# A router on un-normalised sums, ranks summed by TensorE, and weight loads begun ahead of the last norm

## The reference, cut to what matters

```python
h = layer_norm(ALPHA * h + m2 * (mixed @ w_out), ln_mix_g, ln_mix_b)   # post-norm
u = h * (1 + m4) + m3                                                  # modulation
logits = einsum('nd,de->en', u, w_router)       # 16 experts
aff = softmax(logits, axis=experts)
gate, idx = top_k(aff, 64)                      # each expert takes 64 tokens
xe = u[idx]
ye = (silu(xe @ w_g) * (xe @ w_u)) @ w_d * gate
h = layer_norm(ALPHA * h + m5 * scatter_add(idx, ye), ln_ffn_g, ln_ffn_b)
```

## Time and profile before

| | |
|---|---|
| median of 3 runs | 2962.73 us (2961.95 to 2963.7) |
| profiled execution, time | 2959.35 us |
| profiled execution, span | 2957.6 us |
| TensorE busy | 2730.9 us, 92% of the span |
| DVE busy | 1154.3 us, 39% |
| ACT busy | 823.6 us, 28% |
| POOL busy | 126.6 us, 4% |
| mean granted TensorE clock | 0.968 |
| read from memory | 596.90 MB, 203 GB/s over the span |
| chain that ended last | TensorE 75%, DMA 12%, DVE 8%, ACT 4% |

### The profile page before, as it was taken

How to read it: one execution, slowest core, us unless ns; L and a number is a source line. 1 busy time by engine, 2 the same in 40 slices (tenths; PEclk the granted TensorE clock), 3 DMA queues, 4 the chain that set the end, 5 groups by cost and what they waited for, 6 DMA issues and landing times.

```text
span 2957.6 us, 32708 instructions
## 1 busy us (share of the span) xinstructions
PE 2730.9 (92%) x13724; PEld 1797.5 (61%) x13724; DVE 1154.3 (39%) x1684; ACT 823.6 (28%) x1272; POOL 126.6 (4%) x124
## 2 busy tenths in 40 slices
PE   6998899998899979998988999999999999999998
PEld 4555444343368544433337777878778766787886
DVE  4464612111264351111226664323334577533333
ACT  2353311010032121110015424322232467532222
POOL 1210100000000110000001010000010000000000
PEclk8999899999999979999999999999999899999999
DMA  8870699999932079999992112232241300132220
GB/s 299 316 233 16 264 420 426 429 427 421 424 112 103 16 309 427 428 427 427 428 381 87 62 57 95 82 108 72 96 129 41 85 1 1 59 120 78 95 91 36
DMA packets 125651, 601.11 MB, mean 203 GB/s; under 512 B 7440, under 2 KB 12880, under 8 KB 100672
## 3 DMA queue, kind: packets, MB, share of 16 engines
q1 hardware_dynamic: 120128, 584.27, 50.0%
q0 software_dynamic: 5376, 14.75, 1.7%
HBM read 596.90 MB, written 2.10 MB: 203 GB/s over the span
## 4 chain that ended last, share of the span: by engine, by line
PE 75%; DMA 12%; DVE 8%; ACT 4%; issue 1%; POOL 0%; DVEq 0%; SPq 0%; ACTq 0%; POOLq 0%
PE psum L295 72%; DMA weight_ring<-in_w_exp_down 6%; PE psum L310 4%; ACT scratch L283 4%; DVE scratch L245 2%; DMA scratch<-in_w_exp_down 2%; DMA weight_ring<-in_w_exp_up 2%; DMA scratch<-in_w_exp_up 1%; DMA weight_ring<-in_w_mix_in 1%; DVE h L245 1%; DVE scratch L258 1%; DVE scratch L3650 0%; DVE scratch L1408 0%; DVE scratch L1826 0%; DVE scratch L278 0%
## 5 line engine op out<-in xcount | busy, mean ns | idle before, releaser
L295 PE MATMUL psum<-scratch,scratch 128*128 128x512 f32 (+12 forms) x9384 | 1882.0, 398 | 62.9 <-DVE scratch L245 21.8
L295 PEld LDWEIGHTS psum<-scratch,scratch 128*128 128x128 f32 (+3 forms) x9384 | 1380.0, 180 | 529.9 <-issue 207.2
L295 PE MATMUL psum<-weight_ring,scratch 128*64 128x512 f32 (+2 forms) x2752 | 647.5, 610 | 71.3 <-DMA weight_ring<-in_w_exp_down 27.6
L295 PEld LDWEIGHTS psum<-weight_ring,scratch 128*64 128x64 f32 (+2 forms) x2752 | 211.5, 141 | 462.7 <-issue 369.0
L283 ACT ACTIVATE scratch<-psum 128x512 f32<-128x512 f32 (+4 forms) x362 | 210.3, 581 | 999.7 <-PE psum L310 544.3
L245 DVE TENSOR_TENSOR scratch<-weight_ring,scratch 128x2048 fp32r<-128x2048 f32 (+2 forms) x110 | 241.9, 2199 | 485.3 <-ACT scratch L283 483.8
L283 ACT ACTIVATE scratch<-weight_ring 128x2048 fp32r<-128x2048 f32 (+2 forms) x122 | 218.8, 1793 | 571.8 <-PE psum L295 548.6
L245 DVE TENSOR_TENSOR scratch<-scratch,psum 128x512 f32<-128x512 f32 x92 | 63.3, 688 | 521.9 <-PE psum L295 520.4
L245 DVE TENSOR_TENSOR scratch<-scratch,scratch 128x512 fp32r<-128x512 f32 (+12 forms) x355 | 199.1, 561 | 61.5 <-ACT scratch L283 43.0
L310 PE MATMUL psum<-consts,scratch 128*128 128x128 f32 x1116 | 169.6, 294 | 55.5 <-DVE scratch L245 38.9
L310 PEld LDWEIGHTS psum<-consts,scratch 128*128 128x128 f32 x1116 | 135.0, 164 | 116.0 <-issue 48.1
(11 more groups left out here) (106 smaller groups left out, 728.1 us busy)
## 6 DMA issues: line engine op xcount, KB each, us to landing
weight_ring<-in_w_exp_gate SPq DMA_DIRECT2D x44, 2048.0 KB, 15.8
weight_ring<-in_w_exp_down SPq DMA_DIRECT2D x44, 2048.0 KB, 14.2
weight_ring<-in_w_exp_up SPq DMA_DIRECT2D x43, 2048.0 KB, 15.7
weight_ring<-in_ffn_w SPq DMA_DIRECT2D x28, 2048.0 KB, 7.8
weight_ring<-in_w_mod SPq DMA_DIRECT2D x24, 2048.0 KB, 9.5
scratch<-in_w_exp_up SPq DMA_DIRECT2D x21, 2048.0 KB, 16.1
scratch<-in_w_exp_gate SPq DMA_DIRECT2D x20, 2048.0 KB, 15.8
scratch<-in_w_exp_down SPq DMA_DIRECT2D x20, 2048.0 KB, 13.6
```

What stands on the lines that cost most here:

```text
L295: ins = T.eng.matmul(out, lhsT, rhs, start=start, stop=stop)
```

## The change

- **Router on sums.** TensorE turns the un-normalised sum `z` as soon as it stands, half by half, and ACT copies it out plainly (one operation for each half). The gains and the modulation are folded into the router once (`router_dve`), and mean and root are applied to the 16 logits of each token behind the product (`shift_dve`, `logits_dve`). The router is now the stationary operand, 32 columns wide and zero-padded, in four column groups of the array side by side (`logits_pe`); one more small product adds the four groups (`sum_pe`).
- **Order in the mixer.** TensorE turns the tile before between the two output products of a tile. Tile 3's root is taken first and its norm and split only behind the exponential, whose table ACT loads ahead by one small operation. The norm is written to `h`; the parts for the gather are made of the normed tile without gain and bias, and `xeT` is scaled by `turned_scale` and `turned_shift`. Gain and bias of tiles 2 and 3 are applied on DVE in the experts.
- **Ranks.** The marks themselves are transposed; the threshold is on 128x64; a triangle of ones and ones sum them in four products, and a multiplication masks them.
- **Loads.** In layer 0 the first gate pieces go to the two `more` slots at once, without waiting for the mixer's end; the lent slots follow with the first up pieces. In layer 1 the loads still wait for the mixer's end, which now stands ahead of the last norm on ACT and DVE and ahead of the last split on POOL.
- **Halves.** Turning the first gathered rows and the first expert product wait for one half each instead of both.

```diff
@@ MixerOut
     def pe(self, T):
         self.k.fence(T, self.before)
         spread_pe(self.k, T, self.key, self.norm.diag)
         for t in range(NT):
-            project_out_tile(self.k, T, self.key, self.xT, t)
+            project_out_tile(self.k, T, self.key, self.xT, t, halves=(0,))
+            if t == 0:
+                self.next.rows_w_pe(T)
             if t >= 2:
-                self.next.logits_pe(T, t - 2)
+                self.next.sum_pe(T, t - 2)
             if t:
-                self.next.turn_pe(T, t - 1)
+                for q in range(2):
+                    self.next.turn_pe(T, t - 1, q)
+            project_out_tile(self.k, T, self.key, self.xT, t, halves=(1,))
+            if t:
+                self.next.logits_pe(T, t - 1)
+        for q in range(2):
+            self.next.turn_pe(T, NT - 1, q)
+        T.end(self.key)
+        self.next.sum_pe(T, NT - 2)
+        self.next.logits_pe(T, NT - 1)
+        self.next.sum_pe(T, NT - 1)
         if self.rest:
             self.rest.first_pe(T)
-        self.next.turn_pe(T, NT - 1)
-        T.end(self.key)
-        self.next.logits_pe(T, NT - 2)
-        self.next.logits_pe(T, NT - 1)
     def act(self, A):
...
+        for t in range(NT - 1):
+            self.norm.norm_act(A, t)
+            self.next.split_act(A, t)
+            for q in range(2):
+                self.next.turned_out(A, t, q)
+            self.next.part_out(A, t)
+        for q in range(2):
+            self.next.turned_out(A, NT - 1, q)
+        self.norm.root_act(A, NT - 1)
         A.end(self.key)
+        self.next.exp_act(A)
+        self.norm.normal_act(A, NT - 1)
+        self.next.split_act(A, NT - 1)
     def dve(self, V):
...
+        for t in range(NT):
+            self.norm.stats(V, t)
+            if t >= 2:
+                self.next.logits_dve(V, t - 2)
+            if t == NT - 1:
+                V.end(self.key)
+            self.norm.finish(V, t)
+            if t == 0:
+                self.next.rows_w_dve(V)
+            self.next.shift_dve(V, t)
+            if 0 < t < NT - 1:
+                self.norm.gained(V, t - 1)
+        self.next.part_out(V, NT - 1)
+        self.next.logits_dve(V, NT - 2)
+        self.next.logits_dve(V, NT - 1)
     def pool(self, G):
...
         for t in range(NT):
-            self.norm.norm_pool(G, t)
-            if t:
-                self.next.pool_row(G, t - 1)
-        G.end(self.key)
-        self.next.pool_row(G, NT - 1)
+            if t == NT - 1:
+                G.end(self.key)
+            self.next.pool_row(G, t)
+            if t and t < NT - 1:
+                self.norm.norm_pool(G, t - 1)
@@ Experts
-    def turn_pe(self, T, t):
+    def turn_pe(self, T, t, q):
-        T.wait_ge(*k.at(self.before, "norm", t))
+        T.wait_ge(*k.at(self.before, "sum", t, q))
...
-    def fused_dve(self, V):
+    def router_dve(self, V):
...
         tt(V, self.turned_scale, gain, self.scale, ALU.mult)
         tt(V, self.turned_shift, bias, self.scale, ALU.mult)
-        tt(V, self.turned_shift, self.turned_shift, self.shift, ALU.add, (self.key, "fused"))
+        tt(V, self.turned_shift, self.turned_shift, self.shift, ALU.add)
+        fill(V, self.router_w, 0.0)
+        w = self.router_w[:, :, 0:E]
+        tt(V, w, self.router, self.turned_scale.unsqueeze(2).to_broadcast([P, NC, E]), ALU.mult, (self.key, "router"))
+        tt(V, self.router_b, self.router, self.turned_shift.unsqueeze(2).to_broadcast([P, NC, E]), ALU.mult)
+        reduce(V, self.w_sums[:, 0:E], w.rearrange("p c e -> p e c"), ALU.add)
+        reduce(V, self.w_sums[:, E:2 * E], self.router_b.rearrange("p c e -> p e c"), ALU.add, (self.key, "router sums"))
+        V.eng.tensor_tensor_scan(self.triangle, k.ones, k.ident, 0.0, ALU.mult, ALU.add).then_inc(*V.mark((self.key, "triangle")))
+        reduce(V, self.pick, k.ident.rearrange("p (g e) -> p e g", g=4)[:, 0:E, :], ALU.add, (self.key, "pick"))
+    def rows_w_pe(self, T):
...
+        mm(T, bank[:, 0:2 * E], k.ones, self.w_sums, True, True, ("full", key, "rows"))
+    def shift_dve(self, V, t):
+        stt(V, self.shifted[:, t, :], self.w_rows[:, 0:E], self.source.mv[:, t, 1:2], self.w_rows[:, E:2 * E], ALU.mult, ALU.add)
     def logits_pe(self, T, t):
...
+        bank = k.psum.take(T, (key, "part", t), (0, 7))
+        for r in range(2):
+            for g in range(4):
+                c = 4 * r + g
+                mm(T, bank[32 * g:32 * g + 32, 0:P], self.router_w[:, c, :], self.uT[:, t % 2, c, :], r == 0, r == 1,
+                   *([("full", key, "part", t)] if c == NC - 1 else []))
+    def part_out(self, lane, t):
...
+        evac(lane, self.part[:, t % 2, :], k.psum.of((key, "part", t))[:, 0:P], ("free", key, "part", t))
+    def sum_pe(self, T, t):
...
+        mm(T, bank[:, 0:E], self.part[:, t % 2, :], self.pick, True, True, ("full", key, "logits", t))
+    def logits_dve(self, V, t):
...
+        stt(V, self.logits[:, t, :], k.psum.of((key, "logits", t))[:, 0:E], self.source.r[:, t, :], self.shifted[:, t, :],
+            ALU.mult, ALU.add, ("free", key, "logits", t))
     def turned_out(self, lane, t, q):
...
+        evac(lane, self.uT[:, t % 2, 4 * q:4 * q + 4, :], k.psum.of(job).rearrange("p (c n) -> p c n", c=4), ("free", *job))
+    def exp_act(self, A):
+        act(A, self.warm, self.k.ones[:, 0:1], ACT.Exp)
+        A.wait_ge(*self.k.at(self.key, "logits less max"))
+        act(A, self.aff, self.aff, ACT.Exp, (self.key, "exp"))
     def sync(self, Y):
         k, d = self.k, self.k.dram
-        if not self.rest:
+        if self.rest:
+            k.ring.next_in(len(k.ring.base), MORE_SLOTS)
+        else:
             k.ring.widen(Y, self.before)
-        k.ring.lend(Y, self.before)
+            k.ring.lend(Y, self.before)
         for what, e in self.order():
...
+                if self.rest and (name, e) == ("w_exp_up", 0):
+                    k.ring.lend(Y, self.before)
+                    k.ring.next_in(len(k.ring.base) + MORE_SLOTS, LENT_SLOTS)
     def pe(self, T):
...
-        T.wait_ge(*k.at(key, "ranks"))
+        T.wait_ge(*k.at(key, "marked"))
+        bank = k.psum.take(T, (key, "marks"), self.ROUTING)
+        for t in range(NT):
+            tr(T, k, bank[:, t * E:(t + 1) * E], self.work[0:E, t * P:(t + 1) * P],
+               *([("full", key, "marks")] if t == NT - 1 else []))
+        T.wait_ge(*k.at("free", key, "marks"))
         bank = k.psum.take(T, (key, "rank"), self.ROUTING)
-        for t in range(NT):
-            tr(T, k, bank[:, t * E:(t + 1) * E], self.work[0:E, t * P:(t + 1) * P],
+        T.wait_ge(*k.at(key, "triangle"))
+        chosen = self.chosen.rearrange("p t e -> p (t e)")
+        mm(T, bank[:, 0:NT * E], self.triangle, chosen, True, False)
+        for t in range(1, NT):
+            mm(T, bank[:, t * E:NT * E], k.ones, chosen[:, 0:(NT - t) * E], False, t == NT - 1,
                *([("full", key, "rank")] if t == NT - 1 else []))
     def dve(self, V):
...
-        ts(V, work, work, 0.0, None, ALU.is_lt, None)
-        V.wait_ge(*k.at("loaded", f"ones{self.layer}"))
-        V.wait_ge(*V.last())
-        V.eng.tensor_tensor_scan(affT, self.ones[0:E, :], work, 0.0, ALU.mult, ALU.add).then_inc(*V.mark())
-        tt(V, work, work, affT, ALU.mult, (key, "ranks"))
+        V.wait_ge(*k.at("full", key, "marks"))
+        ts(V, self.chosen, k.psum.of((key, "marks"))[:, 0:NT * E].rearrange("p (t e) -> p t e", e=E), 0.0, None, ALU.is_lt, None,
+           ("free", key, "marks"))
         V.wait_ge(*k.at("full", key, "rank"))
-        copy(V, self.rank, k.psum.of((key, "rank"))[:, 0:NT * E].rearrange("p (t e) -> p t e", e=E), ("free", key, "rank"))
+        tt(V, self.rank, k.psum.of((key, "rank"))[:, 0:NT * E].rearrange("p (t e) -> p t e", e=E), self.chosen, ALU.mult,
+           ("free", key, "rank"))
...
         self.turned_dve(V, 0)
+        for t in (NT - 2, NT - 1):
+            self.source.gained(V, t)
...
     def turned_pe(self, T, p):
-        for half in range(2):
-            T.wait_ge(*k.at("free", key, "rows", p, half))
         for q in range(2):
+            T.wait_ge(*k.at("free", key, "rows", p, q))
...
     def up_pe(self, T, e):
-        for q in (range(2) if e in (0, 2, 4, 6) else ()):
-            T.wait_ge(*k.at("free", key, "pair", e // 2, q))
...
+                if w == "w_exp_gate" and c % 4 == 0 and e in (0, 2, 4, 6):
+                    T.wait_ge(*k.at("free", key, "pair", e // 2, c // 4))
```

167 lines of the change are left out of this document (84 added, 83 removed).

## The result

The changed kernel takes 2942.31 us (2940.75 to 2944.66, four runs) against 2962.34 for the kernel before in the same series: ratio on record 0.9942, interval 0.993 to 0.9954 (the quotient of the two medians is 0.9932, so the record's ratio gives the smaller gain). The forecast was 2950.7 and a range of 2944.5 to 2958.5. So the direction was right and the gain, 17 us by that ratio and 20 by the medians, was larger than the 12 forecast. The profiled execution went from a span of 2957.6 to one of 2938.7, 18.9 less.

A forecast was written before the change was run, and what follows sets the result against it. Each expert layer was taken to end when its unbroken train of weight loads ends. Gains of 7.4 us (layer 1) and 4.6 (layer 0) sum to -12.0, giving a median of 2950.7, range 2944.5 to 2958.5.

The forecast's parts named there:

- Ahead of E: Mixer work before E, the end of its last output product: E moves +2.0 us per layer (+1.0 to +3.8).
- E to the stage's end: From the last output product to ACT's root, which releases the loads: 3.05 us.
- E to MAX8: Routing from the last output product to the first MAX8: 8.3 us against 16.8 before.
- Marks to gather: Ranks, from the marks' transposes to the gather's issue: 2.6 us warm, 3.5 cold, 3.8 before; layer 0 loses 1 us waiting.
- Halves: Turning gathered rows by halves takes DVE's copy of half 1 and its latency off the path: -0.8 us.
- Warm gather: Layer 0's first gather product may stay at 2.4 GHz: 0 to -2.5 us.
- First expert product: Start of the experts in both layers: -6.5 - 0.3 - 0.8 = -7.6 us.
- Train of layer 0: Expert weight loads: start 5.2 us earlier, 2.8 dry, dips of 1.0 gone; 3.4 to 6.2, taken as -4.6.
- Train of layer 1: Expert weight loads start at 1046.5 against 1053.90: -7.4 us.
- more than forecast: Rival: router product near 0.5 us and the warm clock give 2946.9 or lower; chance 0.09.
- three signs of failure: E moving over 4 us, TensorE waiting at a turn or sum inside output products, trains running dry again behind 480.
- Only layer 1 gains: Rival: layer 0's dry spell is longer, as when piece 11 or 13 meets a late first expert; 2955.3, chance 0.12.

The follow-up runs named there:

- e1: Changed kernel with layer 0's loads as before: all behind the mixer's end, in the old order of slots; 2942.59 us, ratio 0.9942.
- e2: Changed kernel with layer 0's new order of slots but no loads issued ahead of the mixer's end; 2941.97 us, ratio 0.994.
- f1: Changed kernel with another order of slots in layer 0, so that piece 11 waits for piece 4, not 5; 2941.86 us, ratio 0.9947.
- f3: Changed kernel with extra products that nothing reads in TensorE's pauses of layer 1's routing; 2943.8 us, ratio 0.9957.
- f4: Changed kernel with f1's slots, layer 0's gates ahead of the last modulation pieces, unread products in both layers, layer 1's first three loads early; 2939.58 us, ratio 0.9942.
- e3: Changed kernel with the mixer's end mark back behind tile 3's norm and split; 2949.39 us, ratio 0.9962.
- e6: Changed kernel with both halves awaited before turning and before the first expert product, as before; 2945.6 us, ratio 0.9962.
- e7: Changed kernel with the router product the old way round, without the four column groups, their copy and sum; 2955.05 us, ratio 0.9988.
- e8: Changed kernel with layer 0's modulation product moved behind the four transposes of the affinities; 2942.58 us, ratio 0.9951.
- e5: Changed kernel with the ranks as before: threshold, scan and product on DVE, transposes of the ranks; 2942.52 us, ratio 0.995.
- e4: Kernel before with only layer 0's new order and early issue of loads, without the new mixer; 2960.88 us, ratio 1.0004.

## Why the forecast had the right mechanism and too small a gain

Step by step, with the forecast's terms:

- **Ahead of E, +2.0 us.** Measured +0.3 and +2.6 in the profiled pair, +0.1 and +1.4 in e1. The +1.4 is the clean one: in both kernels all of that stretch is warm, while layer 0 of the kernel before and layer 1 of the kernel after ran their first output product half cold (the latter 8.27 us against 7.0 for the next). The term mis-sized is the router product: 0.58 us for the 16 records, near the lower bound of 0.5, where I took the middle; with it the same sum gives +1.1.
- **E to the stage's end, 3.05 us.** 3.14 and 3.15. Train start of layer 1: 3.3 behind E.
- **E to MAX8, 8.3 us.** 8.38 in layer 1; 9.53 in layer 0. What the sum left out: the modulation product stands ahead of the transposes, and at the low clock it takes 3.53 us. Where it was warm (e2, f1, f3, f4) MAX8 came at some 7.95. The scaling's 0.22 came as foretold.
- **Marks to gather, 2.6 warm and 3.5 cold.** 2.54 and 3.55. The microsecond lost behind the modulation's rest didn't come here, as MAX8 was late itself and the rest warm; it came in e2, f1 and f3, where MAX8 was not late (3.9 us), and for the most part in e1 and e3, where the rest was cold in part (3.35).
- **Halves, -0.8 us.** -1.5 in both (3.97 to 2.49): besides DVE's copy, four transposes instead of eight stand ahead of ACT, and the gap behind it shrank. As e6 shows, it moves the lead and not the length of layer 1.
- **Warm gather, 0 to -2.5.** -2.6 in this execution (6.47 to 3.91), also in e2, e7 and f3, and between +0.3 and -1.1 in the others. No run here shows what decides it.
- **First expert product, -7.6 us.** Against the layer's first output product it came 12.3 us sooner in layer 0 and 6.8 in layer 1, in e1 10.1 and 8.6. The lead, which doesn't hold E's shift, was forecast to fall by 9.6 and fell by 12.5 and 9.4. So layer 1 is as forecast, and of the 2.9 us by which layer 0 beat it, 2.6 are the warm gather.
- **Train of layer 0, -4.6.** -8.2. It was the sum of a start 5.2 earlier, a dry spell of 2.8 and 1.0 of dips gone. The start moved by 7.2 against the first output product, because E moved by 0.3 and not 2.0. The dry spell is real (e3 to e8) and absent here, since the gather was warm: the end of the spread that I had halved, and luck, as the cold gathers of e5, e6 and e8 show. With one of those the layer gains 5.9 to 6.2, still more than 4.6, by the earlier E. What the sum of the prediction took wrongly is small: SP's group of modulation pieces ends at 320.2 with the issue of the last, which itself starts at 319.9.
- **Train of layer 1, -7.4.** -7.4 in the profiled pair, and that it is the same to the tenth is chance: the first piece came 6.6 us sooner against the layer's start, since E was 1.2 late by the cold first product, and 0.8 came behind it. The like runs have 578.4 to 578.9, a gain of 9.7 to 10.2 against this profile of before and 7.6 to 8.1 against e4's layer 1; their first piece came 7.8 sooner (e1).
- **The stage ahead.** 2.9 us of the profiled difference are a clock that the change doesn't touch. The later groups agree with a gain nearer 16 than 20: e1 and e2, e5 and e8, and f1, which differ from the kernel after by little, have medians 17.4, 18.0, 15.9, 15.8 and 16.1 us below the kernel before of their group.

The forecast proper, a gain of 8.5 to 15.5 us with a chance of 0.60, was exceeded. Of the rivals, "more than forecast", with a chance of 0.09, is what happened, by the two terms it named (a product of 0.58 and the warm clock); the second held in this execution and not in most. None of the three signs of failure came: E moved by 2.6 us at most, TensorE waits nowhere between the output products, and behind 480 the DMA engines run without a break as before. POOL's split beside MAX8 cost nothing. Narrow products weren't dear; dear was the old form of the product (e7). "Only layer 1 gains" fell, but its mechanism, the slot wait of piece 11, was the one that decides 2 us of layer 0.

The Trainium skill (TensorEngine Tiling (Array Packing), Key Properties) states that going to another tiling mode drains TensorE. The product of 0.58 us has such a change on both sides; if it costs something, it is within that number. The Trainium skill (SBUF — State Buffer, Who interferes with whom) says that a VectorE instruction with two SBUF inputs and a GpSimd instruction that reads SBUF exclude each other. The trace agrees again: DVE's sum for the first half of tile 3 took 2.79 us at 309.93, beside POOL's addition from 309.81 to 312.17, and the same form for the second half 0.69 at 317.95, alone.

## What to carry to other kernels

Where a stage is an unbroken train of loads through few slots, as in the experts here, its length is fixed (514 us in layer 0), and only its start and its dry spells are to be had. So look for what the first load waits for (here an engine's end mark that stood behind work the loads don't need), and count, load by load, whose use each one then waits for. Start and first consumer must move together: the loads alone (e4) gained nothing, and a consumer alone (e6 against e1, layer 1) gained nothing either. In this kernel, making the operand of 16 columns the stationary one, with column groups side by side, took the product from 1.7 us to 0.58.
